# Starting the expert gathers after the first prompt tile, with the rest of the prompt's attention among them

## The reference, cut to what matters

```python
z = x @ w_in                       # q, k, v of DSA and FoX, index q, k, w, forget logits, two gates
I = sum_h w[t,h] * relu(q_idx[t,h] . k_idx[s]);  keep the top-k keys (128 prompt, 256 sample)
y_a = softmax(q_a . k_a over the kept keys) @ v_a            # DSA, 8 heads, 2 kv heads
y_b = softmax(q_b . k_b + C[t] - C[s]) @ v_b                 # FoX, C = cumsum(log f), 8 heads
h = LN1(ALPHA*x + (sigmoid(g_a)*(y_a @ w_branch_a) + sigmoid(g_b)*(y_b @ w_branch_b)) @ w_out)
q = h @ w_q                        # 8 heads, two halves; scores against 128 sub-keys each
experts = top16 of (top16 of half 0 + top16 of half 1);  gate = softmax(their scores)
x = LN2(ALPHA*h + sum_k gate_k * gelu(u_e . h) * v_e)        # rows of peer_u and peer_v, 16384 x 1024
```

## Time and profile before

| | |
|---|---|
| median of 3 runs | 2809.29 us |
| profiled execution, its span | 2826.42 us, 2824.5 us |
| PE busy | 2085.4 us (74%), 6935 instructions |
| DVE busy | 1804.3 us (64%) |
| POOL busy | 1437.4 us (51%) |
| ACT busy | 405.5 us (14%) |
| HBM read | 810.78 MB, 289 GB/s over the span |
| gathers of peer_u, peer_v | 592 + 592 |

### The profile page before, as it was taken

How to read it: one execution, slowest core, us unless ns; L and a number is a source line. 1 busy time by engine, 2 the same in 40 slices (tenths; PEclk the granted TensorE clock), 3 DMA queues, 4 the chain that set the end, 5 groups by cost and what they waited for, 6 DMA issues and landing times. The chain is left out here.

```text
span 2824.5 us, 24141 instructions
## 1 busy us (share of the span) xinstructions
PE 2085.4 (74%) x6935; PEld 1102.2 (39%) x6940; DVE 1804.3 (64%) x3541; ACT 405.5 (14%) x1065; POOL 1437.4 (51%) x1270
## 2 busy tenths in 40 slices
PE   8982988998888597774868766656787744455676
PEld 6741645687453353322233323332364511112222
DVE  2111555448987858879899755599555489766443
ACT  0111333211010111101010111111101100100110
POOL 0006021000677544557455667656766566777775
PEclk9995579779899799887989998878889877777899
DMA  4112000056999899999989999889999998999997
GB/s 165 52 38 76 1 19 12 35 169 225 346 355 409 307 326 337 337 400 374 400 327 399 399 394 375 329 312 384 369 405 409 386 344 301 322 368 387 354 367 285
DMA packets 259255, 819.23 MB, mean 290 GB/s; under 512 B 32626, under 2 KB 49075, under 8 KB 258291
## 3 DMA queue, kind: packets, MB, share of 16 engines
q0 software_dynamic: 173056, 625.56, 58.7%
q1 hardware_dynamic: 85092, 187.04, 18.5%
q10 hardware_dynamic: 976, 5.10, 0.5%
HBM read 810.78 MB, written 5.65 MB: 289 GB/s over the span
## 5 line engine op out<-in xcount | busy, mean ns | idle before, releaser
L1080 PE MATMUL ps<-arena 128*128 128x512 f32 (+1 forms) x1280 | 736.4, 715 | 385.7 <-DMA arena<-peer_v,arena 285.5
L776 POOL DMA_INDIRECT arena<-peer_u,arena x592 | 694.5, 1173 | 626.1 <-DVE arena L1630 263.6
L1667 DVE CUSTOM_DVE_ANT_0 arena<-arena 128x1024 f32<-128x1024 f32 x592 | 712.7, 1225 | 320.2 <-DMA arena<-peer_u,arena 284.0
L776 POOL DMA_INDIRECT arena<-peer_v,arena x592 | 663.0, 1120 | 384.5 <-issue 163.8
L1080 PEld LDWEIGHTS ps<-arena 128*128 128x128 f32 (+1 forms) x1280 | 256.0, 216 | 808.5 <-issue 707.3
L1676 DVE SCALAR_TENSOR_TENSOR arena<-arena 128x1024 f32<-128x1024 f32 x267 | 343.5, 1286 | 182.0 <-DMA arena<-peer_v,arena 162.8
L934 PE MATMUL ps<-arena 128*128 128x128 f32 (+2 forms) x1152 | 230.9, 363 | 34.2 <-DVE arena L1570 17.9
L934 PEld LDWEIGHTS ps<-arena 128*128 128x128 f32 x1152 | 171.9, 203 | 97.9 <-issue 45.9
L1346 ACT ACTIVATE arena<-arena 128x128 f32<-128x128 f32 (+1 forms) x320 | 114.7, 390 | 535.2 <-PE ps L1080 334.4
L1499 DVE TENSOR_REDUCE arena<-ps 128x1 f32<-128x512 f32 (+4 forms) x80 | 42.4, 531 | 201.2 <-issue 94.0
L1056 PE MATMUL ps<-arena 128*64 128x512 f32 (+1 forms) x512 | 137.7, 462 | 30.7 <-DMA arena<-v_b 25.6
(11 more groups left out here) (166 smaller groups left out, 1914.3 us busy)
## 6 DMA issues: line engine op xcount, KB each, us to landing
arena<-w_mix SPq DMA_DIRECT2D x72, 512.0 KB
arena<-k_b SPq DMA_DIRECT2D x128, 256.0 KB
arena<-v_b SPq DMA_DIRECT2D x128, 256.0 KB
arena<-w_q SPq DMA_DIRECT2D x48, 512.0 KB
arena<-kv_a SPq DMA_DIRECT2D x128, 128.0 KB
arena<-w_out SPq DMA_DIRECT2D x24, 512.0 KB
arena<-peer_u,arena POOLq DMA_INDIRECT x592
arena<-peer_v,arena POOLq DMA_INDIRECT x592
```

The lines of the kernel that those rows point to most:

```text
L776: pool.indirect_dma_start(out=rows[slot_of[n]], out_offset=None, in_=io["peer_v"] if v else io["peer_u"], in_offset=bass.IndirectOffsetOnA ...
L1080: last = pe.matmul(bank(6 + a, 512, 0, nt), diag_p[read_before[n] % ND][:, 0:nt], rows[slot_of[n]][:, a * 512:(a + 1) * 512], start=(k == ...
L1667: dve.tensor_tensor_reduce(out=row, in0=row, in1=h, scale=1.0, scalar=0.0, op0=ALU.mult, op1=ALU.add, accum_out=pre[:, k:k + 1]).then_inc( ...
```

## The change

The second phase barrier goes, and the units become items of the plan.

1. **Order.** `pre_items` now begins with units 0 to 19. Merge 0's items follow, with one unit behind each `mixed`, `norm`, `turn` and every fourth `query`: units 20 to 33. Then the routing of tile 0's first 64 rows, and gather 0. The other 50 steps (units 34 to 79 and the four that drain the pipeline) are put in front of gathers 1 to 80. Merge 1 goes from n = 83 to 238, its routing behind it, the samples' attention from 244 to 708, with gaps of 5 where they were 6. All 32 top-k rounds of the samples now stand at n = 86 to 449.
2. **POOL.** The 16 forget gathers wait for merge 0's mixing (`mix_done`), index groups 0 and 1 for the scan of the forget values (`tail_ready`), which moves behind query 7 of merge 0. Groups 2 and 3 stand in the queue in front of gathers 20 and 27. Gather 0 also waits for merge 0's last key scores.
3. **Memory.** The attention's buffers stay alive among the gathers, so the ring has 7 slots up to n = 84, 9 up to n = 732, 15 behind. Heads are kept in two halves of the partitions (`head`), and FoX's bias, which was a 65th row of the keys, comes from `negc` through an own matmul with 8 rows for each fox unit. Merge 0 and merge 1 have weight buffers of their own.
4. **PSUM.** Attention takes banks 0 to 3 (two for scores, one for the transposes, one for the product, where it had eight; the wide scores of tile 4 also use 4 and 5), merge 0 takes 4 to 7 with single buffers.
5. **SP.** The first four weights are issued before the phase barrier; the small loads come behind it, after x and the norm's rows. xT is loaded again after the third group of index keys is used, merge 1's weights when all units are done.
6. **Value rows of tile 0.** PE takes every second, where it took every fourth.

The core of the diff:

```diff
-        TOP_0 = 12
-        pre_items = [("admit",)]
-        for n, (item, _) in enumerate(merge_items(0)):
+        STEPS = NU + 4
+        FIRST = 20
+        pre_items = [("unit", u) for u in range(FIRST)]
+        u = FIRST
+        for item, _ in merge_items(0):
             pre_items.append(item)
-            if item[0] == "mixed":
-                pre_items.append(("top", item[2]))
-        pre_items += [("top", r_) for r_ in range(KD, TOP_0)]
+            if item[0] in ("mixed", "norm", "turn") or item[0] == "query" and item[2] % 4 == 3:
+                if item == ("mixed", 0, KD - 1):
+                    pre_items.append(("ones",))
+                if item == ("query", 0, 7):
+                    pre_items.append(("tail",))
+                pre_items.append(("unit", u))
+                u += 1
...
+        U_TO, M1_TO = 82, 238
+        unit_at, left = {}, STEPS - u
+        for j in range(left):
+            unit_at[u + j] = 1 + (U_TO - 1) * j // left
+            put(unit_at[u + j], "unit", u + j)
...
-        n_top = ROUNDS_S - TOP_0
-        top_from, top_to = m1_end + 50, q_at_[("s_max", 3)]
+        put(U_TO + 2, "admit")
+        top_from, top_to = U_TO + 4, q_at_["s_max", 3]
...
-        SWITCH = s_end + 24
+        SWITCH = (0, U_TO + 2, s_end + 24)
...
             if i == 0:
-                return k % 4 != 3
+                return k % 2 == 1
...
+            pool.wait_ge(lidx_ready, 1)
+            pool.wait_ge(mix_done, KD)
             for j in range(NPG):
                 pool.indirect_dma_start(out=lp[:, j * 128:(j + 1) * 128], out_offset=None, in_=io["logf_b"],
...
+            pool.wait_ge(tail_ready, 1)
+            index_pages(0)
+            index_pages(1)
             for n, (i, v, k) in enumerate(gathers):
+                for c in (2, 3):
+                    if n == sidx_at[c - 2] + 10:
+                        index_pages(c)
...
+                elif slot_of[n] == 0:
+                    pool.wait_ge(sc_ready, 4)
                 elif slot_of[n] == NR0:
+                    pool.wait_ge(o_copied, NU)
+                elif slot_of[n] == NR1:
                     pool.wait_ge(se_ready, NB)
...
+                        if fox is not None:
+                            last = pe.matmul(out, ident[0:NH, fox:fox + 1].to_broadcast([NH, nq]), negc[:, c0:c1],
+                                             start=False, stop=not biased)
...
                     pe.wait_ge(diag_ready, u + 1)
-                    if u >= 2:
-                        pe.wait_ge(pt_copied, u - 1)
+                    if u:
+                        pe.wait_ge(pt_copied, u)
...
+                for w in range(NMW, 48):
                     weights(w)
...
+                sp.wait_ge(s_ready, use_no["sia", 3, 1] + 1)
+                sp.dma_start(xT[:], io["xT"]).then_inc(xT_loaded, 16)
+                sp.wait_ge(o_copied, NU)
+                for w in range(48, 2 * 48):
+                    weights(w)
...
-            prompt()
-            end_phase(dve, 2)
+            prompt_start()
             for kind, *at in plan:
-                if kind == "admit":
+                if kind == "unit":
+                    prompt_step(*at)
+                elif kind == "ones":
+                    dve.memset(ones, 1.0).then_inc(lf_ones, 1)
+                elif kind == "tail":
+                    tail_sums()
+                elif kind == "admit":
                     admit()
```

More of the change, by code:

```diff
@@ L296, in program @@
         lng4, lnb4 = r.take(D), r.take(D)
-        rows += [r.take(D) for _ in range(NR - NR0)]
-        r = Region(mw_at)
+        NR = NR1 + (a_end - r.at) // D
+        rows += [r.take(D) for _ in range(NR - NR1)]
+        r = Region(mw_at, b_at)
         h_twice, h_eight = r.take(D), r.take(D)
@@ L445, in sample_items @@
             out = [(("zero",), 0), (("spread", 0), 1)]
-            out += [(("s_score", 0, c), 6) for c in range(5)]
+            out += [(("s_score", 0, c), 5) for c in range(5)]
             out += [(("s_max", 0), 2), (("s_exp", 0), 2), (("s_norm", 0), 2), (("s_turn", 0), 3)]
@@ L535, in program @@
         newest, fills = {}, {}
+        slots = (NR0, NR1, NR)
         for n, d in enumerate(by_dve):
@@ L538, in program @@
             n_dve, n_pe = n_dve + d, n_pe + (not d)
-            s_ = n % NR0 if n < SWITCH else (n - SWITCH) % NR
+            j = sum(n >= at for at in SWITCH) - 1
+            s_ = (n - SWITCH[j]) % slots[j]
             last_in.append(newest.get(s_))
```

549 lines of the change are left out of this document (298 added, 251 removed).

## The result

| | before | after |
|---|---|---|
| median of the runs, us | 2808.82 (2806.84 to 2816.41, 4 runs) | 2846.27 (2840.77 to 2852.39, 4 runs) |
| profiled execution, us | 2826.42 | 2841.18 |
| its span, us | 2824.5 | 2839.4 |

The ratio is 1.0143, with a 95% interval of 1.0104 to 1.0182: the kernel became slower by some 40 us (the medians are 37 apart). The forecast was 2780 and faster, with 2840 as the upper end of its range. So of the 66 us between forecast and measurement, 44 are in the sum of stages (2839.4 against 2795.5), 22 in how the two profiled executions stand to their medians.

The account below looks back on a forecast made before the run. PE with its handshakes was taken to bound before the first gather, transfers behind it. Stages 460 + 272 + 393 + 1670.5 = 2795.5 against a span of 2824.5: 29 less, so 2809.3 - 29 = 2780 us; range 2700 to 2840.

Parts of the forecast that it names:

- First gather at 460: Head of the kernel: the first expert gather goes out at 460 us (442 to 475), against 701.2 before.
- Unit stage, 272: Gathers 0 to 84, beside the moved attention units: 272 us (228 to 330), DVE 90% busy, PE nearly as full.
- The 14 us for the index pages: Unit stage: the last two index pages, 16 gathers each in POOL's queue, hold the units 7 us each.
- Rival B: Unit stage: PE's half clock sets it; at mean clock 0.55 it takes 327 us, total 2835; chance 17%.
- the rule that busy means fast: Unit stage: a busy PE gets 2.4 GHz, leaving the stage to DVE alone, 6 us less; the prediction set it aside.
- Merge stage, 393: Gathers 84 to 238: PE bounds the merge work at 393 us (365 to 410), DVE and DMA hidden.
- seams and norms (16): Merge stage: 7 us to reload xT and four weights, 9 us for PE waiting on three norms.
- Rest, 1670.5: The last 946 gathers, behind gather 238: 1645.5 us as before plus 25 for later sample work.
- 8 page fills of 1.05: Rest: 48 sample slots now behind gather 238, about 8 page fills of 1.05 MB, cost 25 us.
- Rival C: Handshakes run free and DVE alone bounds the unit stage: 442 and 245, 45 us less, about 2731; chance 22%.
- D: Transfers bound everything from the first gather: the first 238 gathers take 478 us, not 665, total 2593; chance 4%.
- E: Behind gather 238 the shorter ring and the later sample take another 25 us: about 2805; chance 15%.

Follow-up runs that it names:

- e4: The kernel before with POOL's 64 small gathers issued four at a time, each four after a further unit, not in strings of 16; ratio 0.9781.
- e5: The changed kernel with POOL's 80 small gathers spread: 40 in fours, the other 40 one by one behind expert gathers; ratio 0.9952 to the kernel before.
- e13: The changed kernel, strings of gathers kept, with DVE reading three of four value rows of the first tile, not one of two; ratio 1.0015 to the kernel before.
- e6: e4 with one more unread 128x128 by 512-column f32 product on PE in each of the first 56 unit steps; ratio 0.9817 to the kernel before.
- e8: e4 with 160 small writes of zeros on POOL, one after the other, once the 60th unit is computed; one run, 2753.02 us.
- e12: e4 with its small gathers in twos, not fours, at the same mean rate; ratio 0.9794 to the kernel before.
- e1: The changed kernel with one more unread 512-column f32 product on PE in each of the 46 unit steps beside the gathers; ratio 1.0149 to the kernel before.
- e2: The changed kernel with a second pair of PSUM banks for transposes and results of odd units from 36 on; ratio 1.0101 to the kernel before.
- e7: The changed kernel without two of five key blocks in transposes and value products of each 16-row-tile unit; ratio 1.0045 to the kernel before.
- e11: e9 with units laid out over 76 gathers, not 82, and merging and routing up to gather 210, not 238; ratio 0.9960 to the kernel before.
- e17: e16 with none of the sample's top-8 rounds due between gathers 238 and 320, laid before and behind instead; ratio 0.9790 to the kernel before.
- e10: e5 with DVE reading seven of eight value rows of the first tile, not one of two; ratio 0.9816 to the kernel before.
- e15: e10 with two unread 512-column bf16 products on PE in each unit step from 60 on; ratio 0.9876 to the kernel before.
- e16: e10 with gathers before the first expert gather in twos, only two of the second index page's there; ratio 0.9838 to the kernel before.
- e9: e5 with DVE reading three of four value rows of the first tile, not one of two; ratio 0.9845 to the kernel before.

## Why the prediction was wrong

- **First gather at 460**: 461.9, right. Units 0 to 19 took 217 to 270 us with one interval over 5 us, of 6.2, where the prediction had said none (e4 shows that the hold of late signals was the cause of before's 58.6 us), and the gaps came back under the index pages of the head: from 386.7 one maximum of DVE to the next took 46 us, under the string that ends at 422.
- **Unit stage, 272: this step failed.** It took DVE at 90% (252) as the bound, let PE's 228 lie beside it for 6 us more, and added 14 for the index pages. DVE's work was 238, close to the 227. PE's was too: 184 us at full clock against 180. But the clock was .66, so PE was busy 278 us, not 228, which rested on the 0.78 of the prompt's attention in before; and PE stood idle for 51 us more in handshakes, which the step had not counted. 278 + 51 = 329. Of the 51 us, 46 lie ahead of 609 us, where the first wait follows the hold of the head. The 14 us for the index pages fit e5's 13, which is one pair of profiles.
- **Rival B** named the mechanism and its time, 327. But it reached that from a mean clock of 0.55 and no idle time; its own threshold, a clock under 0.60, was not met. It had the right cause and two errors that cancelled. I gave it 17% although the prediction itself quoted 50.6 us at half clock with PE full as evidence against the rule that busy means fast. The weight should have followed from that row.
- **Merge stage, 393**: 362, PE 345 busy at a clock of .97, DMA .84. PE bound it as said, and was 32 us quicker than its terms by form: busy 345 us against 377. It was idle for 17 us, which is what had been put down for seams and norms (16). The DMA share was above the 0.8 that I had named. The split of the value rows stood in the sum (half of 103 us) but was never asked about alone; e13 shows that it is the difference between slower and no change.
- **Rest, 1670.5: this step failed too**, by more than its 1686.4 shows. Kernels that hold the same instructions behind gather 238 took 1618 to 1646 us there in the order of before (before, e4, e6, e8, e12; middle value 1635) and 1686 to 1702 in the changed order (after, e1, e2, e5, e7; 1697). So the order costs some 62 us here, where 25 were forecast; the profile of before is the longest of its five here and that of after the shortest. With the 26 us that the profiles gain ahead of gather 238 (1178.8 to 1153) this makes 36 us, near the 37 to 40 measured, where the two spans alone make 15.
  - By place it is 44 us in gathers 238 to 320 (161 to 205), 20 in gathers 320 to 440 (246 to 266), and nothing behind them.
  - In the first of these the bytes hardly differ (62 and 64 MB), and the DMA share falls from 1.01 to 0.87. What was added is DVE's work, and it is tile 1's routing. The plan puts all its 16 steps in front of gathers 240 to 276; before they stood ahead of gather 238. I had moved them with merge 1 and priced them nowhere. The top-8 rounds there are as many as they were, 8 and 7. The sums and DVE's groups, first before, then after, and what POOL waited for:

```profile
1178.80:1339.80 161.00, 108.42 (x265) 43.85 (x264) 134.75 (x168) 13.01 (x25) 107.68 (x83) 0.82 1.01 384
L1526 DVE MAX8 arena<-arena 64x8 f32<-64x2056 f32 x8 | 18.4, 2299 | 0.3
POOL arena L776 <- DVE arena L1667: 7.4, 3, 3.7
```

```profile
1153.00:1358.00 205.00, 127.48 (x361) 58.00 (x359) 180.51 (x408) 19.19 (x43) 103.32 (x82) 0.82 0.87 314
L1621 DVE MAX8 arena<-arena 64x8 f32<-64x2056 f32 x7 | 16.1, 2299 | 0.2
L1725 DVE TENSOR_TENSOR arena<-arena 128x512 f32<-128x512 f32 x8 | 5.6, 694 | 0.3
POOL arena L859 <- DVE arena L1764: 44.9, 12, 6.1
```

  - L1725 is one of the routing's lines; together they are some 65 us in this stretch, and before has none of them there. e11 moved half of the routing out and e17 the rounds (20 and 27 us of DVE), and the stretch shortened by 21 and 16. That DVE bounds it is so supported from two sides; moving the routing alone was not tried.
  - In gathers 320 to 440 the DMA share is 1.00 in after and 5 MB more are moved, 14 us at 381 GB/s, so here the later sample is the likely cause. Behind gather 238 as a whole 614 MB are moved, not 601: 13 MB more, where the prediction took 8 page fills of 1.05.
- **Rival C** (handshakes free) and **D** (transfers bound everything) had no support. **E** had the right place and not the cause: it took the shorter ring and the later sample, and most of the loss is the routing on DVE.
- In sum: the head gained 9 us (701.2 - 230.5 - 461.9) where 11 were forecast, unit and merge stage 17 (230.5 + 478 - 691) in place of 43, and the rest takes 41: 15 us more, the difference of the spans.
- Three slips in the prediction's figures changed nothing in its forecast: the DMA digit is 5 and 6 in slices 9 and 10 and reaches 8 or 9 from slice 11 (counted from 1); the first gather's upper bound by its own terms is 470 and not 475; rival C's 45 us less make 2735 and not 2731.

What is still open: why the granted clock stays at .50 in the small products, and how gathers issued back to back delay what other engines read, and how much of the rest's 62 us comes back if tile 1's routing stays ahead of gather 238. Of the first two the runs show the effect and its price, not its inside.

Two routes end at the same time. The kernel before with its gathers in fours (e4, 2756 us) or twos (e12, 2744) and the changed order with paced gathers, value rows given to DVE and moved rounds (e17, 2763) have ratios of 0.978 to 0.979. All three beat the kernel before by about 2%, and the changed one by about 3.5%. The simplest is e4: two added waits.

## What to carry to other kernels

When work is moved from beside one neighbour to beside another, ask of the busiest engine what clock it had in the stretch that supplies its durations, and add its waits: a sum of busy time at another clock is not a bound. Price every piece of work that moves (here 32 rows on PE, and 16 routing steps on DVE) in the stage where it lands, with the row that says how full that engine is there. And when a gap is found in the kernel before, try to remove it there first: two waits gave 62 us, as much as the reordering with pacing and its split of rows mended (e17, 59).

## What the runs showed of the hardware

- While 48 gathers were issued back to back by GpSimd (0.94 us each, 0.30 between), PE, ACT and DVE got 4 units done in 58.6 us; with the same gathers in fours it was 20. Fours and twos could not be told apart. Beside 160 small writes of the same engine, in 26 us, the units kept their pace.
- TensorE stayed at 1.2 GHz for 109 us while it was busy 104.2 of 109.6 us, mostly in products with 16 rows or 16 columns. The Trainium skill (TensorE: Matmul & The Clock Gate, Part 1) ties the clock to how busy the engine has been; here busy and slow stood side by side again. Added 512-column f32 products raised it (.66 to .78 in e1, .74 to .87 in e6), added bf16 ones did not (.62 in both e10 and e15), and none of these kernels was faster for it.
- The same instructions up to gather 84, in one execution each of e16 and e17, were granted .70 and .63 in the unit stage and took 302 and 325 us for it. With the same products of the units, e5, e9 and e10 lie between (.65, .68, .69; 316, 305, 305 us).
